# Both heads' transposes and the values at the end of a unit, the second head's blocks in the values' PSUM bank

## Chip, cores and metric

The kernel runs on one core of one Trainium2 chip. The metric is the device time of one execution in microseconds (us), the median of three runs: 1748.26 us for the kernel before. The time of the kernel after is measured in the same way.

## What is computed

A two-layer hybrid encoder takes one step on 512 new prompt frames and 32 sample frames. In each layer one large input projection feeds three branches (a gated convolution, a gated token mixer and stick-breaking attention), their outputs are merged, and a gated feed-forward part follows. The change touches the attention alone:

```python
def stick_breaking(q, k, v, q_pos, k_pos):
    z = jnp.einsum('bqhd,bkhd->bhqk', q, k, preferred_element_type=jnp.float32) * (SB_HEAD_DIM ** -0.5)
    mask = k_pos[None, :] < q_pos[:, None]
    log_keep = jnp.where(mask, jax.nn.log_sigmoid(-z), 0.0)
    later = lax.cumsum(log_keep, axis=3, reverse=True) - log_keep
    attn = jnp.where(mask, jnp.exp(jax.nn.log_sigmoid(z) + later), 0.0)
    return jnp.einsum('bhqk,bkhd->bqhd', attn.astype(v.dtype), v)

def stick_breaking_prompt(q, k, v):
    ...
    for i in range(seq // SB_QBLOCK):
        lo, hi = i * SB_QBLOCK, (i + 1) * SB_QBLOCK
        outs.append(stick_breaking(q[:, lo:hi], k[:, :hi], v[:, :hi], pos[lo:hi], pos[:hi]))
    return jnp.concatenate(outs, axis=1)
```

A prompt has four query blocks of 128 rows, and block i sees i + 1 key blocks. There are eight heads of width 64. The kernel works on them in four pairs.

## The kernel before

**The main work.** TensorE multiplies activations by weight chunks. Each float32 product is made from a high and a low part, so each tile takes three matmuls: high by high, low by high, high by low (lines 2046, 2051 and 2052, in the helper `three_of`). A *unit* is one accumulation into one of the four PSUM banks `acc0` to `acc3`: 8 tiles by 3 matmuls, 24 matmuls of 272 columns. A *chunk* of weights gives four units (function `chunk`, which calls `unit`). The helper `unit` calls `mid` after its first 12 matmuls, and `chunk` calls `end` after a unit's last one.

**Attention hidden between units.** In each layer, five chunks in a row (20 units, n = 0 to 19) carry the attention. One *step* is one query block of one pair of heads: 16 steps, where step n belongs to pair n // 4 and has n % 4 + 1 key blocks of 128. Then two steps for the sample rows follow. A step goes through the engines as follows:

- TensorE, `scores(n)` at the end of unit n: the scores of both heads into the banks `score0` and `score1` (line 2122).
- ScalarE, `sigmoids(n)` in unit n + 1: two sigmoids for each head, `keep` and `beta` (lines 644 and 645). Every second step has its `beta` in the buffer that is called `gex`.
- GpSimd masks the diagonal block, two instructions for each head (line 543).
- VectorE, `made(n)` in unit n + 1: for each head a scan along `keep` (line 1347) and a product into `beta` (line 1350), which signals `at_full` of that head.
- TensorE, `turns(n, part)` in unit n + 2: transposes of the first head's blocks (`part` 0) in the middle of the unit, in `within`, and of the second head's (`part` 1) at its end, in `behind`. Both go to one PSUM bank, `turned` (`bt`, line 2153), so part 1 waits for ScalarE's copy of part 0 (`att_full`).
- ScalarE, `turned(n, part)`: copies out of that bank into `att` and `late` (lines 663 and 666).
- TensorE, `values(ht)`, once for each pair of heads, in the middle of the units n = 6, 10, 14 and 18: eight matmuls into the whole bank `small` (`bo`, 512 columns, line 2173).
- ScalarE, `out_rows(ht)`, right behind its first copy of that unit: copies `small` to the high part of the branch's result (line 681).
- VectorE, `rows_lo(ht)`, in unit n = 7, 11, 15 and 19: reads `small` once more for the low part (line 1370) and signals `yc_full`. In units 7, 11 and 15 it stands in VectorE's queue behind `made(6)`, `made(10)` and `made(14)`, both heads of a step with three blocks; the function `attend` sets that order. The next `values` waits for `yc_full`, since it writes the same bank.

**What sets the order.** Each engine's order is written out by hand, and an engine takes its instructions in that order. A wait on a semaphore holds up all that stands behind it on its engine. On TensorE that is everything: the units, the transposes and the scores are one queue.

Of the kernel before, what the change touches and what calls it, by code (L numbers as in the profile page):

```python
# [8 lines left out]
ACT = mybir.ActivationFunctionType  # L9
AX_X = mybir.AxisListType.X  # L10

P = 128
# [9 lines left out]
CT = CH // P  # L22
# [116 lines left out]
def trunk(nc, adds, x_in, win, wbr, wout, wup, wdn, par_in, bc_in, sguw_in, kc_in, vc_in, gh_in, fh_in,  # L139
          y_out, k_out, v_out, glu_out, ffn_out, sgu_out):  # L140
    with ExitStack() as ctx:
        sems = {}

        def sem(name):
            sems[name] = ctx.enter_context(nc.semaphore(name))
            return sems[name]
# [4 lines left out]
        def sb(name, shape, dt=F32, at=None):  # L151
            size = 4
            for s in shape[1:]:
                size *= s
            off = at
            if at is None:
                off = top[0]
                top[0] += (size + 31) // 32 * 32
            return nc.alloc_sbuf_tensor_at(name, shape, dt, offset=off)
# [9 lines left out]
        ident = sb("ident", [P, P])  # L169
# [70 lines left out]
        beta = [[sb(f"beta0{i}", [P, T], at=C + i * 2176) for i in range(2)],  # L240
                [gex[:, i, 4:GEX] for i in range(2)]]
# [16 lines left out]
        bt = ctx.enter_context(nc.psum_tensor("turned", [P, 512], F32))  # L258
        bo = ctx.enter_context(nc.psum_tensor("small", [P, 512], F32))
# [29 lines left out]
        at_full = [sem(f"at_full{i}") for i in range(2)]  # L289
        t_full = sem("t_full")  # L290
        att_full = [sem(f"att_full{i}") for i in range(2)]
        o_full = sem("o_full")
        o_hi = sem("o_hi")
        yc_full = sem("yc_full")
# [69 lines left out]
        STEPS = 16  # L364
        ALL = STEPS + 2

        def dcol(h):
            return slice(h * HALF, (h + 1) * HALF)
# [3 lines left out]
            return gex[:, b // 2, 4 + b % 2 * HALF:4 + (b % 2 + 1) * HALF]  # L372

        cbank = (bo, bt)
        PA, PB, PC = (ps[0], ps[1]), (bs[0], bs[1]), (bo, bt)

        def bank_of(q, p):
# [196 lines left out]
        def _(act):  # L574
            c = Count()
# [80 lines left out]

            def turned(n, part):

                act.wait_ge(t_full, c.take(t_full))
                if n < STEPS:  # L660
                    i = n % 4
                    early = min(i + 1, 2)
                    ins = A(att[part][:, i:i + 3 * early - 2:3, :],
                            bt[:, 0:early * P].rearrange("p (a n) -> p a n", a=early), ACT.Copy)
                    if i > 1:
                        ins = A(late[part][:, i - 2:2 * i - 3, :],
                                bt[:, 2 * P:(i + 1) * P].rearrange("p (a n) -> p a n", a=i - 1), ACT.Copy)
                    ins.then_inc(att_full[part], c.up(att_full[part]))
                elif part == 0:
                    s = n - STEPS  # L670
                    A(att[s][:, 0:4, :], bt[:, 0:PAST].rearrange("p (a n) -> p a n", a=4), ACT.Copy).then_inc(
                        att_full[s], c.up(att_full[s]))
                else:
                    s = n - STEPS
                    A(att[s][0:DEC, 4, :], bt[0:DEC, 0:P], ACT.Copy).then_inc(att_full[s], c.up(att_full[s]))

            def out_rows(ht):

                act.wait_ge(o_full, c.take(o_full))
                if ht < CT:  # L680
                    A(yc[0][:, ht, 0:SEQ], bo[:, :], ACT.Copy).then_inc(o_hi, c.up(o_hi))
                else:
                    A(yc[0][:, :, SEQ:T], bo[:, 0:P].rearrange("p (a n) -> p a n", a=CT), ACT.Copy).then_inc(
                        o_hi, c.up(o_hi))
# [5 lines left out]
                    sigmoids(n - 1)  # L690

            def within(n):
                if 2 <= n < ALL + 2:
                    turned(n - 2, 0)
                if 6 <= n <= STEPS + 2 and n % 4 == 2:
                    out_rows((n - 6) // 4)

            def behind(n):
                if 2 <= n < ALL + 2:
                    turned(n - 2, 1)  # L700

            def plain(dst, m, b, sig_to, fn=ACT.Copy):

                h = b // 2
                act.wait_ge(acc_full[b], c.take(acc_full[b]))
                A(dst[:, m, dcol(h)], ps[b][:, 0:HALF], fn).then_inc(acc_free[b], c.up(acc_free[b]))
# [1318 lines left out]
        def _(pe):  # L2025
            c = Count()
            mm = pe.matmul
            turn = [0]
            turned_by = [None]
# [11 lines left out]
            def three(out, s, at, xs, start, stop):  # L2041
                return three_of(out, (wh[s][:, at:at + P], wl[s][:, at:at + P]), xs, start, stop)
# [98 lines left out]
            def turn_bank():  # L2141
                if turned_by[0] is not None:
                    pe.wait_ge(turned_by[0], c.seen(turned_by[0]))

            def turns(n, part):
# [15 lines left out]
                c.skip(att_full[s])  # L2161
                turned_by[0] = att_full[s]

            def values(ht):

                for b in range(2):
                    pe.wait_ge(att_full[b], c.seen(att_full[b]))
                pe.wait_ge(yc_full, c.prev(yc_full))
                for kb in range(4):
                    for b in range(2):  # L2170
                        h = 2 * ht + b
                        blocks = (att[b][:, 0:4, :], att[b][:, 4:7, :], late[b][:, 0:2, :], late[b][:, 2:3, :])[kb]
                        last = mm(bo[DH * b:DH * b + DH, kb * P:SEQ], vtok[:, kb, h * DH:(h + 1) * DH],  # L2173
                                  blocks.rearrange("p a n -> p (a n)"), start=kb == 0, stop=kb == 3)
                last.then_inc(o_full, c.up(o_full))
# [18 lines left out]

            def within(n):

                if 6 <= n <= STEPS + 2 and n % 4 == 2:
                    values((n - 6) // 4)
                if 2 <= n < ALL + 2:
                    turns(n - 2, 0)  # L2200

            def behind(n):
                if 2 <= n < ALL + 2:
                    turns(n - 2, 1)
                if n == ALL + 2:
                    sample_values()
                if n < ALL:
                    scores(n)
# [16 lines left out]
            for r in range(DEPTH):  # L2225
# [8 lines left out]
                if r == 0:  # L2234
# [4 lines left out]
                    for t in range(KT):  # L2239
# [3 lines left out]
                        for b in range(2):  # L2243
                            last = three(ps[b][:, 0:HALF], s0, t * 256 + b * P, [x[:, t, dcol(0)] for x in xs],
                                         t == 0, t == KT - 1)
# [57 lines left out]
                for n in range(5):  # L2303
                    if n == 2:
                        qk_out[8] = out_of()
                    chunk(mid=lambda b, n=n: within(4 * n + b), end=lambda b, n=n: behind(4 * n + b))
# [10 lines left out]
                def last_values(b):  # L2317
                    if b == 0:
                        behind(STEPS + 4)
                    turn_first(b)  # L2320
# [81 lines left out]
                blocks = {}  # L2402
# [160 lines left out]
```

## Time and profile before

| | |
|---|---|
| median of 3 runs | 1748.26 us (1747.83 to 1748.93) |
| the profiled execution | 1748.06 us, of it 1746.3 us span |
| TensorE matmul busy | 1732.0 us, 99% of the span |
| VectorE busy | 1331.6 us, 76% |
| ScalarE busy | 850.4 us, 49% |
| GpSimd busy | 122.6 us, 7% |

The span is what the trace covers, and 1.8 us of the execution lie around it. Busy times of one engine can be added; those of different engines overlap. A start time in the rows below counts from the start of the span. A matmul's printed duration is how long it is in the engine; matmuls overlap, so what one costs TensorE is the distance from its start to the start of the next.

### The profile page before, as it was taken

To read this page: it belongs to the slowest core of one execution; us is meant where nothing else is said; L and a number is where in the kernel's file an instruction comes from. 1 tells how busy PE (TensorE), PEld (TensorE's weight loads), DVE (VectorE), ACT (ScalarE), POOL (GpSimd) and SP (SyncE) were. 2 spreads that over 40 slices of the span, in tenths; PEclk is the share of its full clock that TensorE was granted. 3 is DMA by queue.
4 is the path that set the end of the run, shared out by engine and by line. 5 is a ranking of instruction groups with operands and counts; after the bars stand their busy time and mean duration, and the time that the engine had idled before them with its cause. 6 is when DMAs were issued, how large, how long until landed. Compare 5 with 4: busy or idle time off the path is not lost.

```text
span 1746.3 us, 32655 instructions
## 1 busy us (share of the span) xinstructions
PE 1732.0 (99%) x13802; PEld 1697.1 (97%) x13802; DVE 1331.6 (76%) x1903; ACT 850.4 (49%) x1388; POOL 122.6 (7%) x167
## 2 busy tenths in 40 slices
PE   9999999999999999999999999999999999999997
PEld 9998899999999999999999989999999999999997
DVE  5698778664779999876667887777457799998675
ACT  4246532363366655644542565233535556656443
POOL 0025100000030000000000350000001200000000
PEclk9999999999999999999999999999999999999999
DMA  5432132222213223355524221223232222223544
GB/s 177 156 117 74 37 97 75 74 88 94 87 66 114 97 97 100 107 181 176 169 96 156 93 73 62 75 85 96 74 99 95 73 97 97 97 99 131 176 163 136
DMA packets 36513, 185.99 MB, mean 107 GB/s; under 512 B 7376, under 2 KB 11728, under 8 KB 18192
## 3 DMA queue, kind: packets, MB, share of 16 engines
q1 hardware_dynamic: 34672, 176.28, 30.1%
q10 hardware_dynamic: 1696, 7.64, 1.3%
q8 instruction: 109, 1.79, 0.4%
q14 instruction: 36, 0.29, 0.1%
HBM read 176.75 MB, written 7.15 MB: 105 GB/s over the span
## 4 chain that ended last, share of the span: by engine, by line
PE 95%; DVE 3%; issue 1%; DMA 0%; ACT 0%; ACTq 0%; DVEq 0%
PE acc L2046 23%; PE acc L2052 23%; PE acc L2051 23%; PE score L2046 5%; PE score L2052 5%; PE score L2051 5%; PE turned L2051 1%; PE turned L2052 1%; PE score L2122 1%; PE turned L2046 1%; PE small L2051 1%; PE small L2052 1%; PE small L2046 1%; PE small L2173 1%; PE turned L2153 1%; DVE acc L1402 1%
## 5 line engine op out<-in xcount | busy, mean ns | idle before, releaser
L2046 PE MATMUL acc<-xh,wh 128*128 128x272 f32 x1928 | 564.9, 293 | 1.4 <-DVE xl L1152 1.2
L2052 PE MATMUL acc<-xh,wl 128*128 128x272 f32 x1928 | 555.4, 288 | 0.0
L2051 PE MATMUL acc<-xl,wh 128*128 128x272 f32 x1928 | 554.9, 288 | 0.0
L2046 PEld LDWEIGHTS acc<-xh,wh 128*128 128x128 f32 x1928 | 363.1, 188 | 9.1 <-issue 5.4
L1198 DVE TENSOR_TENSOR wl<-raw,wh 128x2048 fp32r<-128x2048 f32 (+2 forms) x118 | 236.1, 2001 | 174.0 <-ACT wh L586 173.4
L2051 PEld LDWEIGHTS acc<-xl,wh 128*128 128x128 f32 x1928 | 363.2, 188 | 0.1
L2052 PEld LDWEIGHTS acc<-xh,wl 128*128 128x128 f32 x1928 | 362.2, 188 | 0.0
L586 ACT ACTIVATE wh<-raw 128x2048 fp32r<-128x2048 f32 (+2 forms) x138 | 236.5, 1714 | 163.8 <-DMA raw<-wdn 116.8
L2046 PE MATMUL acc<-fhh,wh 128*128 128x272 f32 x704 | 204.1, 290 | 0.0
L2052 PE MATMUL acc<-fhh,wl 128*128 128x272 f32 x704 | 202.5, 288 | 0.0
L2051 PE MATMUL acc<-fll,wh 128*128 128x272 f32 x704 | 202.4, 287 | 0.0
L1402 DVE SCALAR_TENSOR_TENSOR acc<-glu,par,acc 128x574 f32<-128x574 f32 x240 | 181.1, 814 | 0.1
L864 ACT ACTIVATE tmp<-acc,par 128x272 f32<-128x272 f32 x96 | 46.7, 488 | 195.1 <-PE acc L2052 194.8
L2046 PEld LDWEIGHTS acc<-fhh,wh 128*128 128x128 f32 x704 | 132.6, 188 | 0.4
L2051 PEld LDWEIGHTS acc<-fll,wh 128*128 128x128 f32 x704 | 132.5, 188 | 0.2
L2052 PEld LDWEIGHTS acc<-fhh,wl 128*128 128x128 f32 x704 | 132.3, 188 | 0.0
L2046 PE MATMUL score<-th,shi 128*128 128x272 f32 x288 | 83.9, 291 | 0.0
L2052 PE MATMUL score<-th,slo 128*128 128x272 f32 x288 | 83.2, 289 | 0.0
L2051 PE MATMUL score<-tl,shi 128*128 128x272 f32 x288 | 82.5, 287 | 0.0
L2046 PE MATMUL acc<-mh,wh 128*128 128x272 f32 x256 | 74.8, 292 | 0.0
L2052 PE MATMUL acc<-mh,wl 128*128 128x272 f32 x256 | 73.7, 288 | 0.0
L2051 PE MATMUL acc<-ml,wh 128*128 128x272 f32 x256 | 73.7, 288 | 0.0
(321 smaller groups left out, 3883.7 us busy)
## 6 DMA issues: line engine op xcount, KB each, us to landing
raw<-win SPq DMA_DIRECT2D x50, 1024.0 KB, 5.0
raw<-wup SPq DMA_DIRECT2D x44, 1024.0 KB, 5.0
raw<-wdn SPq DMA_DIRECT2D x32, 1024.0 KB, 4.9
raw<-wbr SPq DMA_DIRECT2D x24, 512.0 KB, 3.7
raw<-wdn SPq DMA_DIRECT2D x16, 768.0 KB, 4.2
raw<-wout SPq DMA_DIRECT2D x8, 1024.0 KB, 5.1
v_out<-vfm ACTq DMA_DIRECT2D x2, 1088.0 KB, 9.3
k_out<-k ACTq DMA_DIRECT2D x2, 1088.0 KB, 4.9
```

The lines of the kernel that those rows point to most:

```text
L586: A(wh[s][:, 0:n], raw[s][:, 0:n], ACT.Copy).then_inc(hi_full[s], c.up(hi_full[s]))
L864: A(tmp[:, b, :], ps[b][:, 0:HALF], ACT.Sigmoid, bias=col(par, PAR["b_gate"] + 8 * BRANCHES[n] + 2 * i + b % 2)).then_inc(acc_free[b], c.u ...
L1198: v.tensor_tensor(wl[s][:, 0:n], raw[s][:, 0:n], wh[s][:, 0:n].bitcast(F32), ALU.subtract).then_inc(lo_full[s], c.up(lo_full[s]))
L1402: v.scalar_tensor_tensor(out=acc[:, m, :], in0=glu_at(m, j), scalar=w, in1=acc[:, m, :], op0=ALU.mult, op1=ALU.add).then_inc(vec, c.up(vec))
L2046: first = mm(out, a, xs[0], start=start, stop=False, skip_group_check=onto)
L2051: mm(out, a, xs[1], start=False, stop=False, skip_group_check=onto)
L2052: return mm(out, b, xs[0], start=False, stop=stop, skip_group_check=onto)
L2122: last = mm(bs[b][:, 0:w], yc[x][rows, ht, i * P:w], ks[y][rows, ht, 0:w], start=x + y == 0, stop=y == 1)
L2153: last = pe.transpose(bt[:, kb * P:(kb + 1) * P], beta[n % 2][part][:, kb * P:(kb + 1) * P], ident[:, :])
L2173: last = mm(bo[DH * b:DH * b + DH, kb * P:SEQ], vtok[:, kb, h * DH:(h + 1) * DH], blocks.rearrange("p a n -> p (a n)"), start=kb == 0, sto ...
```

## The change

Three things change, in the steps of the prompt (n < 16):

- On TensorE the new function `both_turns` transposes the blocks of both heads, one behind the other, at the end of the unit. The middle of a unit is empty, except in the units 18 and 19. `values` of the pairs 0, 1 and 2 moves from the middle to the end of its unit, ahead of `both_turns`. The last pair's `values` and the sample steps stay in the middle of their units.
- The second head's blocks go to another place: for a step with one block to the second quarter of `turned`, for a step with two, three or four blocks to `small`, the bank of the values (`second_bank`). Before these blocks TensorE waits until `yc_full` has reached the number of the `values` issued so far, the wait `pe.wait_ge(yc_full, c.seen(yc_full))`. The wait for the copy of the first head's blocks between the two heads falls away.
- On ScalarE `turned` of both heads and `out_rows` of the pairs 0 to 2 move to the end of the unit, behind the copies of the unit's own result. Where both heads' blocks lie in one bank, the first copy waits for both heads' transposes.

VectorE's, GpSimd's and SyncE's instructions and their orders are as before.

```diff
             return gex[:, b // 2, 4 + b % 2 * HALF:4 + (b % 2 + 1) * HALF]
 
         cbank = (bo, bt)
+
+        def second_bank(blocks):
+            return (bt, P) if blocks == 1 else (bo, 0)
+
         PA, PB, PC = (ps[0], ps[1]), (bs[0], bs[1]), (bo, bt)
 
         def bank_of(q, p):
@@ -656,15 +660,16 @@
 
             def turned(n, part):
 
-                act.wait_ge(t_full, c.take(t_full))
+                act.wait_ge(t_full, c.take(t_full) + (1 if n < STEPS and n % 4 == 0 and part == 0 else 0))
                 if n < STEPS:
                     i = n % 4
                     early = min(i + 1, 2)
+                    bank, at = second_bank(i + 1) if part else (bt, 0)
                     ins = A(att[part][:, i:i + 3 * early - 2:3, :],
-                            bt[:, 0:early * P].rearrange("p (a n) -> p a n", a=early), ACT.Copy)
+                            bank[:, at:at + early * P].rearrange("p (a n) -> p a n", a=early), ACT.Copy)
                     if i > 1:
                         ins = A(late[part][:, i - 2:2 * i - 3, :],
-                                bt[:, 2 * P:(i + 1) * P].rearrange("p (a n) -> p a n", a=i - 1), ACT.Copy)
+                                bank[:, 2 * P:(i + 1) * P].rearrange("p (a n) -> p a n", a=i - 1), ACT.Copy)
                     ins.then_inc(att_full[part], c.up(att_full[part]))
                 elif part == 0:
                     s = n - STEPS
@@ -690,14 +695,18 @@
                     sigmoids(n - 1)
 
             def within(n):
-                if 2 <= n < ALL + 2:
+                if STEPS + 2 <= n < ALL + 2:
                     turned(n - 2, 0)
-                if 6 <= n <= STEPS + 2 and n % 4 == 2:
-                    out_rows((n - 6) // 4)
+                if n == STEPS + 2:
+                    out_rows(CT - 1)
 
             def behind(n):
+                if 2 <= n < STEPS + 2:
+                    turned(n - 2, 0)
                 if 2 <= n < ALL + 2:
                     turned(n - 2, 1)
+                if 6 <= n < STEPS + 2 and n % 4 == 2:
+                    out_rows((n - 6) // 4)
 
             def plain(dst, m, b, sig_to, fn=ACT.Copy):
 
@@ -2161,6 +2170,23 @@
                 c.skip(att_full[s])
                 turned_by[0] = att_full[s]
 
+            def both_turns(n):
+
+                blocks = n % 4 + 1
+                for part in range(2):
+                    pe.wait_ge(at_full[part], c.take(at_full[part]))
+                    if part == 0:
+                        turn_bank()
+                    elif blocks > 1:
+                        pe.wait_ge(yc_full, c.seen(yc_full))
+                    bank, at = second_bank(blocks) if part else (bt, 0)
+                    for kb in range(blocks):
+                        last = pe.transpose(bank[:, at + kb * P:at + (kb + 1) * P],
+                                            beta[n % 2][part][:, kb * P:(kb + 1) * P], ident[:, :])
+                    last.then_inc(t_full, c.up(t_full))
+                    c.skip(att_full[part])
+                turned_by[0] = att_full[1]
+
             def values(ht):
 
                 for b in range(2):
@@ -2194,13 +2220,17 @@
 
             def within(n):
 
-                if 6 <= n <= STEPS + 2 and n % 4 == 2:
+                if n == STEPS + 2:
+                    values(CT - 1)
+                if STEPS + 2 <= n < ALL + 2:
+                    turns(n - 2, 0)
+
+            def behind(n):
+                if 6 <= n < STEPS + 2 and n % 4 == 2:
                     values((n - 6) // 4)
-                if 2 <= n < ALL + 2:
-                    turns(n - 2, 0)
-
-            def behind(n):
-                if 2 <= n < ALL + 2:
+                if 2 <= n < STEPS + 2:
+                    both_turns(n - 2)
+                if STEPS + 2 <= n < ALL + 2:
                     turns(n - 2, 1)
                 if n == ALL + 2:
                     sample_values()
```

The change moves instructions, so here is what stands in TensorE's queue at the end of the first pair of heads, in the first layer. Units 6 and 7 before (`acc` is a unit's own work, cut here; `beta` is step 4, `gex` step 5):

```order
L2052 MATMUL acc<-xh,wl_58 128x272
L2173 MATMUL small<-att_141,vtok 64x512 [waits yc_full,att_full1,att_full0]
...
L2153 MATMUL turned<-ident,beta_139 128x128 [waits att_full1,at_full0]
L2046 MATMUL acc<-xh,wh_52 128x272
...
L2153 MATMUL turned<-ident,beta_140 128x128 [waits att_full0,at_full1]
L2122 MATMUL score<-ksh,ych 128x384 [waits sig_full1,sig_full0]
...
L2153 MATMUL turned<-ident,gex 128x128 [waits att_full1,at_full0]
...
L2153 MATMUL turned<-ident,gex 128x128 [waits att_full0,at_full1]
...
L2122 MATMUL score<-ksh,ych 128x512 [waits sig_full1,sig_full0]
```

The same place of the changed kernel, whose line numbers are higher:

```order
L2199 MATMUL small<-att_141,vtok 64x512 [waits yc_full,att_full1,att_full0]
...
L2184 MATMUL turned<-ident,beta_139 128x128 [waits att_full1,at_full0]
L2184 MATMUL turned<-ident,beta_140 128x128 [waits at_full1]
L2131 MATMUL score<-ksh,ych 128x384 [waits sig_full1,sig_full0]
...
L2184 MATMUL turned<-ident,gex 128x128 [waits att_full1,at_full0]
L2184 MATMUL turned<-ident,gex 128x128
L2184 MATMUL small<-ident,gex 128x128 [waits yc_full,at_full1]
L2184 MATMUL small<-ident,gex 128x128
L2131 MATMUL score<-ksh,ych 128x512 [waits sig_full1,sig_full0]
```

The values and all transposes now stand between a unit's last matmul and the scores, and the second head's transposes of unit 7 write `small` behind a wait for `yc_full`.

ScalarE's queue from the end of unit 5 to the sigmoids of step 6, before:

```order
L645 ACTIVATE gex<-score 128x256
L663 ACTIVATE att_141<-turned 128x128 [waits t_full]
L681 ACTIVATE ych<-small 128x512 [waits o_full]
L796 ACTIVATE qd<-acc 128x32 [waits acc_full2]
L798 ACTIVATE ych<-acc 128x240
L663 ACTIVATE att_142<-turned 128x128 [waits t_full]
L644 ACTIVATE keep_137<-score 128x384 [waits at_full0,s_full0]
```

and in the changed kernel:

```order
L649 ACTIVATE gex<-score 128x256
L805 ACTIVATE qd<-acc 128x32 [waits acc_full2]
L807 ACTIVATE ych<-acc 128x240
L668 ACTIVATE att_141<-turned 128x128 [waits t_full]
L668 ACTIVATE att_142<-turned 128x128 [waits t_full]
L686 ACTIVATE ych<-small 128x512 [waits o_full]
L648 ACTIVATE keep_137<-score 128x384 [waits at_full0,s_full0]
```

Both copies of step 4 and the copy of `small` now stand right ahead of the sigmoids of step 6.

VectorE's queue, the same in both kernels, at the same place:

```order
L1347 SCALAR_TENSOR_TENSOR keep_137<-keep_137,zero 128x384 [waits mask_full0]
L1350 TENSOR_TENSOR beta_139<-beta_139,keep_137 128x384 [waits vec]
L1347 SCALAR_TENSOR_TENSOR keep_138<-keep_138,zero 128x384 [waits mask_full1]
L1350 TENSOR_TENSOR beta_140<-beta_140,keep_138 128x384 [waits vec]
L1370 TENSOR_TENSOR ycl<-small,ych 128x512 [waits o_hi]
```

The read of `small` stands behind both heads of step 6.

## Rows read from the trace of the kernel before

**Rows 1.** The page: busy time by engine, and granted TensorE clock in 40 slices.
```profile
PE 1732.0 (99%) x13802; PEld 1697.1 (97%) x13802; DVE 1331.6 (76%) x1903; ACT 850.4 (49%) x1388; POOL 122.6 (7%) x167
PEclk9999999999999999999999999999999999999999
```
**Rows 2.** Waits of PE alone: line, releaser, total us, times, longest us.
```profile
PE acc L2046 <- DVE xl L1152: 1.2, 2, 1.0
```
**Rows 3.** PE timeline, unit 2's middle (start us, us, instruction): one transpose.
```profile
116.07 0.29 PE L2052 MATMUL acc<-xh,wl 128*128 128x272 f32 x1
...
116.44 0.28 PE L2051 MATMUL acc<-xl,wh 128*128 128x272 f32 x1
116.56 0.29 PE L2052 MATMUL acc<-xh,wl 128*128 128x272 f32 x1
```
**Rows 4.** PE timeline, ends of units 1 (no transpose) and 2 (one transpose).
```profile
113.83 0.29 PE L2052 MATMUL acc<-xh,wl 128*128 128x272 f32 x1
114.05 0.39 PE L2122 MATMUL score<-ksh,ych 64*128 64x256 f32 x2
...
117.69 0.29 PE L2052 MATMUL acc<-xh,wl 128*128 128x272 f32 x1
117.82 0.27 PE L2153 MATMUL turned<-ident,beta 128*128 128x128 f32 x1
118.02 0.44 PE L2122 MATMUL score<-ksh,ych 64*128 64x384 f32 x2
```
**Rows 5.** PE timeline, unit 5: four transposes in the middle, four at the end.
```profile
129.12 0.29 PE L2052 MATMUL acc<-xh,wl 128*128 128x272 f32 x1
...
129.81 0.28 PE L2051 MATMUL acc<-xl,wh 128*128 128x272 f32 x1
...
131.06 0.30 PE L2052 MATMUL acc<-xh,wl 128*128 128x272 f32 x1
...
131.73 0.38 PE L2122 MATMUL score<-ksh,ych 64*128 64x256 f32 x2
```
**Rows 6.** PE timeline, unit 6: values and one transpose in its middle.
```profile
133.75 0.29 PE L2052 MATMUL acc<-xh,wl 128*128 128x272 f32 x1
133.97 1.72 PE L2173 MATMUL small<-att,vtok 128*64 128x512 f32 x8
...
136.27 0.33 PE L2153 MATMUL turned<-ident,beta 128*128 128x128 f32 x1
...
136.56 0.28 PE L2051 MATMUL acc<-xl,wh 128*128 128x272 f32 x1
```
**Rows 7.** PE timeline: scores of step 6, then the transposes at unit 7's end.
```profile
138.14 0.44 PE L2122 MATMUL score<-ksh,ych 64*128 64x384 f32 x2
...
142.21 0.38 PE L2153 MATMUL turned<-ident,gex 128*128 128x128 f32 x2
```
**Rows 8.** DVE timeline in unit 7: scans of step 6, and the read of `small`.
```profile
140.89 1.02 DVE L1347 TENSOR_TENSOR_SCAN keep<-keep,zero 128x384 f32<-128x384 f32 x1 [1.85 <-POOL beta L543]
...
143.88 0.68 DVE L1370 TENSOR_TENSOR ycl<-small,ych 128x512 fp32r<-128x512 f32 x1
```
**Rows 9.** PE timeline, the same place of unit 11.
```profile
162.38 0.38 PE L2153 MATMUL turned<-ident,gex 128*128 128x128 f32 x2
```
**Rows 10.** DVE timeline, the read of `small` in unit 11.
```profile
163.95 0.68 DVE L1370 TENSOR_TENSOR ycl<-small,ych 128x512 fp32r<-128x512 f32 x1
```
**Rows 11.** ACT timeline, unit 6 into unit 7: copies, and the first sigmoid.
```profile
136.63 0.28 ACT L663 ACTIVATE att<-turned 128x128 f32<-128x128 f32 x1 [2.83 <-PE turned L2153]
136.81 0.59 ACT L681 ACTIVATE ych<-small 128x512 fp32r<-128x512 f32 x1
...
138.97 0.49 ACT L644 ACTIVATE keep<-score 128x384 f32<-128x384 f32 x1 [0.20 <-PE score L2122]
```
**Rows 12.** PE timeline at the start: TensorE's longest wait.
```profile
9.99 0.36 PE L2046 MATMUL acc<-xh,wh 128*128 128x272 f32 x1 [0.99 <-DVE xl L1152]
```
**Rows 13.** DVE timeline at the start: the instruction that ended that wait.
```profile
9.12 0.72 DVE L1152 TENSOR_TENSOR xl<-xT,xh 128x544 fp32r<-128x544 f32 x1
```

More of the change, by code:

```diff
@@ L2195, in within @@
             def within(n):
-                if 6 <= n <= STEPS + 2 and n % 4 == 2:
-                    values((n - 6) // 4)
-                if 2 <= n < ALL + 2:
+                if n == STEPS + 2:
+                    values(CT - 1)
+                if STEPS + 2 <= n < ALL + 2:
                     turns(n - 2, 0)
             def behind(n):
-                if 2 <= n < ALL + 2:
+                if 6 <= n < STEPS + 2 and n % 4 == 2:
+                    values((n - 6) // 4)
+                if 2 <= n < STEPS + 2:
+                    both_turns(n - 2)
+                if STEPS + 2 <= n < ALL + 2:
                     turns(n - 2, 1)
```

## Prediction

> **What bounds the kernel now.** I read the page first. TensorE is busy for 1732.0 us, 99% of the span of 1746.3 us, and its granted clock reads full in all 40 slices [rows 1]. Then TensorE's waits: its largest row is 1.2 us in two waits at the start [rows 2], the three rows under it are smaller, and none is at a transpose of attention, at the values or at the scores of L2122. So the kernel is TensorE's queue. A us less of work in it is a us gained, a wait put into it is a us lost, and no later wait is there that could give it back. VectorE, at 76%, counts only where TensorE waits for it. The third view is the timeline of TensorE through the attention units, to see what a transpose costs in the middle of a unit and at its end. The last is the timelines of VectorE and ScalarE in units 6 and 7, where the new wait stands.
>
> **What the moved transposes give.** Two successive matmuls of a unit start 0.12 to 0.13 us apart, I take 0.125 [rows 3]. In the middle of unit 2 one transpose stands between an L2052 and the next but one matmul, which come 116.44 - 116.07 = 0.37 us apart instead of 0.25: it costs 0.12 us. Four transposes in unit 5 cost 129.81 - 129.12 - 0.25 = 0.44 us [rows 5]. At a unit's end the distance to the scores is 0.22 us with no transpose and 0.33 us with one [rows 4], 0.67 us with four [rows 5]: 0.11 and 0.45 us. So a block costs 0.11 us in either place, and breaking into a unit costs next to nothing beyond that: 0.01 us or less. There are 16 steps in each of 2 layers, 32 breaks, so this gives 0 to 0.3 us; I take 0.2 us.
>
> The values cost 136.56 - 133.75 - 0.25 = 2.56 us in the middle of unit 6 with their one transpose [rows 6]. At the end, the same eight pairs take 136.27 - 133.97 = 2.30 us, the way in is 0.22 us instead of the 0.13 us that a transpose there has (117.69 to 117.82, [rows 4]), and the transpose is 0.11 us: 2.50 us. That gives 0.06 us for each of 6 (three pairs of heads, two layers), 0.4 us. The gain on TensorE is 0.6 us in all, with bounds of 0 and 1.0 us.
>
> The dropped wait for ScalarE's copy between the heads gives nothing, since TensorE did not wait at a transpose [rows 2]. ScalarE's copies that now come later are wanted by TensorE a whole unit later (about 3 us), when the values or the next first-head transposes need them; that unit hides them.
>
> **What the new wait costs.** This is the large term. The second head's transposes of a step with two or more blocks write `small`, so they wait for `yc_full`, for VectorE's read of the values (L1370). The first such step behind a `values` is in the next unit: values in unit 6, transposes of step 5 (two blocks) at the end of unit 7. Before, that bank had until the next `values`, in unit 10. VectorE's place for the read is unchanged: behind both scans and products of step 6. These start only when the scores of step 6 have been through ScalarE and GpSimd; VectorE itself waits 1.85 us for that in unit 7 [rows 8]. So the read can't come earlier because TensorE waits; it hangs on scores that TensorE issued one unit before.
>
> Measured in the trace of before: the scores of step 6 start at 138.14 and the transposes at unit 7's end at 142.21 [rows 7]. In the changed kernel the second head's transposes would come at the same distance from the scores, since the two transposes that leave the unit's middle stand in front of them now. The read ends at 143.88 + 0.68 = 144.56 [rows 8]. TensorE is 144.56 - 142.21 = 2.35 us too early. In unit 11 it is 163.95 + 0.68 - 162.38 = 2.25 us [rows 9, 10]. The other four places (unit 15, and units 7, 11 and 15 of the second layer) repeat this, with 2.24, 2.24, 2.25 and 2.24 us. Sum of six: 13.6 us.
>
> Two things are added at each place. First, ScalarE: the last transpose of unit 6 starts 0.20 us ahead of the scores [rows 4]; the copy behind it starts 0.36 us later (136.27 to 136.63, [rows 6, 11]), that is at scores + 0.16. Then come 0.18 us for one copy, 0.18 us for the other head's, and the copy of `small`, 0.59 us, of which about 0.1 us overlaps with the next instruction (as 136.63 + 0.28 runs past 136.81, [rows 11]). The first sigmoid starts at scores + 1.01 us; before it started at 138.97 - 138.14 = 0.83 us. All behind it, GpSimd's masks, the scans and the read, is 0.18 us later. Bounds: 0 (if the overlap is larger) and 0.3 us. Second, TensorE's start after VectorE's end, which no transpose shows; the nearest row is the wait at the start, where VectorE ends at 9.12 + 0.72 = 9.84 and TensorE starts at 9.99 [rows 12, 13]: 0.15 us. The Trainium skill, "Advanced Engine Details and Errata", section Network/Comms, gives 50 to 100 ns for reading a semaphore; by that the sum would be 0.3 to 0.6 us smaller, and the row decides. Bounds from the rows: 0 and 0.3 us, since the printed 0.68 us of the read may hold some of it.
>
> So a place costs 2.68 us in unit 7 of the first layer and about 2.58 us in the five others, 13.6 + 6 x 0.33 = 15.6 us in all. Behind the waiting transpose stand the scores of step 7 and all the units, so nothing on TensorE covers it.
>
> **Sum.** 1748.06 us (the profiled execution, 1746.3 us of it span; 0.2 us under the median) - 0.6 + 15.6 = 1763.1 us; I say 1763.0 us, 0.84% slower. With all bounds at one end: -1.0 + 13.6 = +12.6, 1760.7 us; at the other: 0 + 13.6 + 6 x 0.6 = +17.2, 1765.3 us.
>
> **Rivals.**
>
> *The clock falls.* TensorE would stand still for some 2.6 us six times, and in this trace it never waits over 1.2 us [rows 2], around which the clock reads full [rows 1]. So no row shows what such a pause does. If the engine went from 2.4 to 1.2 GHz for about a unit behind each pause, 24 matmuls at 0.125 us more, 3.0 us, would be added six times: 1763 + 18 = 1781 us. For one pause alone it is 1766 us. Against it stands that each pause is short beside the full work around it. The Trainium skill, "TensorE: Matmul & The Clock Gate", section "HAM oscillation", has idle stretches between bursts of matmuls bring the lower clock back; no row here bears it out. Chance 0.10.
>
> *No wait, so not slower.* If VectorE's read had ended before TensorE reaches the bank, only the gain would be left: 1748.1 - 0.6 = 1747.5 us, no difference that can be measured. The mechanism would be a read that goes ahead of the scans of step 6, or sigmoids that start much sooner because the ScalarE queue is shorter in the middle of unit 7. It decides at 142.21: the read would have to end 2.35 us sooner. VectorE's queue has not changed, and it already waits for GpSimd there [rows 8]. The same result comes about if the wait asks for a lower count than I read. Chance 0.04.
>
> *A second wait behind the first.* After the pause the scores of step 7 (four blocks) come 2.6 us late, and their transposes stand at the end of unit 9. From the scores of step 6 to the end of its products is 143.88 - 138.14 = 5.7 us [rows 7, 8], for four blocks about 1.1 us more by the width of its instructions, 6.9 us. TensorE needs two units of 3.1 us, two sets of scores and six transposes, about 8.3 us. The slack of 1.4 us covers it. If it were gone, up to 1 us at each of six places would be added: 1769 us. Chance 0.05.
>
> **How the numbers follow.** The forecast of 1763 us, bounds 1760 to 1766, has 0.80. The clock has 0.10, the second wait 0.05, no wait 0.04, and 0.01 is left for a gain that I don't see. A measurement of this kernel tells a difference of about 0.2% (3.5 us) from none. Slower by more than that: 0.80 + 0.10 + 0.05 = 0.95. Within it: 0.04. Faster: 0.01. The range goes from 1757 (waits shorter than the rows' lower bound) to 1770 us (it takes in the second wait and a lower clock after one or two pauses), and leaves out the clock's full price and the case of no wait.
>
> **What would show it.** In the profile of the changed kernel TensorE's waits should have a row for the transposes into `small`, released by VectorE L1370, six times (more with lesser ones), about 15 us in total, 2.7 us at most. VectorE's scan of step 6 should still wait for GpSimd, and the read end about 0.2 us later against the scores than before. A unit without a break should take 24 matmuls at 0.125 us. The granted clock should stay full in every slice; a lower digit in slices 4, 5, 24 or 25 is the first rival. If the transposes into `small` show no wait, the reading of the counts or of VectorE's order was wrong, and if the pauses are there but the time is not, something on TensorE was cheaper without the breaks than the distances in [rows 3 to 6] say.

## The result, and the profile after

The changed kernel takes 1774.01 us (median of 4 runs, 1771.91 to 1776.71) against 1748.6 us, a ratio of 1.0149 (95% interval 1.0137 to 1.0161). It is slower by 25.4 us, where 14.9 us was forecast, and it lies outside the range that was given. Its profiled execution took 1774.42 us, 1772.7 us of it span; that is 26.4 us more span than before. A few executions of the versions below, and of the kernel before beside them, took 2022 to 4341 us; they are left out of every median and ratio here.

The page of the kernel after, busy time by engine and granted TensorE clock in 40 slices, answers to [rows 1]:

```profile
PE 1743.2 (98%) x13802; PEld 1704.9 (96%) x13802; DVE 1331.3 (75%) x1903; ACT 848.3 (48%) x1388; POOL 115.6 (7%) x167
PEclk9999999999999999999999998999999999999999
```

TensorE has the same 13802 matmuls and is busy for 11.2 us longer. So the loss is not idle time alone: the same work took longer. A single 8 stands in the row of the clock, in the 25th slice. A slice is 44 us wide and a 9 stands for 90% or more, so the row is too coarse for the sign that the prediction named: slices 4, 5 and 24 read 9, though the clock was low for 3.4 us in each of them, twice in the 4th, as the stretches further down show.

TensorE's waits (line, releaser, total us, times, longest us), which answer to [rows 2]:

```profile
PE small L2184 <- DVE ycl L1379: 14.2, 6, 2.5
PE acc L2055 <- DVE xl L1161: 1.8, 2, 1.5
```

The first row is the forecast wait: the transposes into `small` (L2184), released by VectorE's read (now L1379), six times. The second row is the wait at the start that was there before, 0.6 us longer in this execution. One small row further down matters for the account at the end, a single wait for a weight chunk at 735 us, which the kernel before did not have in its trace:

```profile
PE score L2055 <- DVE wl L1814: 0.4, 1, 0.4
```

The timeline of TensorE from the end of unit 7 into unit 8 (start us, us, instruction), which answers to [rows 7]:

```profile
142.25 0.29 PE L2061 MATMUL acc<-xh,wl 128*128 128x272 f32 x1
142.38 0.38 PE L2184 MATMUL turned<-ident,gex 128*128 128x128 f32 x2
145.22 0.41 PE L2184 MATMUL small<-ident,gex 128*128 128x128 f32 x2 [2.46 <-DVE ycl L1379]
145.56 0.70 PE L2131 MATMUL score<-ksh,ych 64*128 64x512 f32 x2
...
148.11 0.43 PE L2060 MATMUL acc<-xl,wh 128*128 128x272 f32 x1
148.34 0.43 PE L2061 MATMUL acc<-xh,wl 128*128 128x272 f32 x1
...
149.31 0.28 PE L2060 MATMUL acc<-xl,wh 128*128 128x272 f32 x1
149.44 0.29 PE L2061 MATMUL acc<-xh,wl 128*128 128x272 f32 x1
...
150.96 0.29 PE L2061 MATMUL acc<-xh,wl 128*128 128x272 f32 x1
```

The first head's two transposes take 0.22 us from 142.38. The second head's could start at 142.60 and start at 145.22: a pause of 2.62 us. At 148.11 two matmuls of a unit are 0.23 us apart, at 149.31 they are 0.13 us apart again. Both are the same instruction; between them the clock has come back.

The same seen as stretches (stretch, then its length, busy time of each engine with instructions in brackets, granted clock, DMA share, GB/s), the first six at or behind the end of the six pauses and the last elsewhere:

```profile
core 0: us, PE busy (x) PEld busy (x) DVE busy (x) ACT busy (x) POOL busy (x), PEclk, DMA share, GB/s
145.70:149.10 3.40, 3.40 (x15) 2.66 (x16) 0.57 (x3) 2.31 (x6) 0.54 (x2) 0.50 0.22 34
169.60:173.00 3.40, 3.40 (x15) 2.43 (x14) 1.09 (x2) 1.88 (x5) 0.27 (x2) 0.50 0.07 12
193.50:196.90 3.40, 3.34 (x13) 2.29 (x14) 1.36 (x2) 1.46 (x4) 0.00 (x0) 0.50 0.00 0
1020.80:1024.20 3.40, 3.40 (x25) 2.83 (x26) 1.16 (x3) 2.45 (x6) 0.54 (x2) 1.00 0.26 36
1043.40:1046.80 3.40, 3.32 (x13) 2.27 (x14) 1.39 (x2) 1.43 (x4) 0.00 (x0) 0.50 0.02 5
1067.30:1074.10 6.80, 6.50 (x27) 5.46 (x28) 3.81 (x6) 4.24 (x6) 2.23 (x4) 0.50 0.40 126
1098.00:1101.40 3.40, 3.40 (x19) 3.36 (x17) 3.33 (x5) 0.28 (x1) 0.00 (x0) 0.50 0.00 0
```

A clock of 0.50 is 1.2 GHz, 1.00 is 2.4 GHz. At five of the six pauses the clock went to the low level, at one of those for twice as long; after the pause in unit 7 of the second layer (1020.80) it stayed full. Compare the instructions in equal stretches: 15 matmuls at half clock, 25 at full. The stretch at 1098.00 follows no pause. Ahead of it stand 3.3 us of the sample rows' small matmuls, 32 columns each, which TensorE has in every version.

### The profile page after: what moved, and what is told of

Same layout as the page of the kernel before. It is cut to its first block, busy times and chain, and to the rows that moved or that the text cites. A ratio compares the mean times of both kernels' runs of the same rounds, so it can differ in the third digit from the quotient of the medians.

```text
span 1772.7 us, 32647 instructions
## 1 busy us (share of the span) xinstructions
PE 1743.2 (98%) x13802; PEld 1704.9 (96%) x13802; DVE 1331.3 (75%) x1903; ACT 848.3 (48%) x1388; POOL 115.6 (7%) x167
## 4 chain that ended last, share of the span: by engine, by line
PE 92%; DVE 4%; ACT 1%; issue 1%; DMA 1%; POOL 0%; ACTq 0%; DVEq 0%; POOLq 0%
PE acc L2055 22%; PE acc L2061 22%; PE acc L2060 22%; PE score L2055 5%; PE score L2061 4%; PE score L2060 4%; PE turned L2060 1%; PE turned L2061 1%; PE score L2131 1%; PE turned L2055 1%; PE small L2060 1%; PE small L2061 1%; PE small L2055 1%; PE small L2199 1%; DVE acc L1411 1%
## 5 line engine op out<-in xcount | busy, mean ns | idle before, releaser
L1356 DVE TENSOR_TENSOR_SCAN keep<-keep,zero 128x128 f32<-128x128 f32 (+4 forms) x68 | 58.3, 857 | 37.9 <-POOL gex L547 18.7
```

The lines of the kernel that those rows point to most:

```text
L1356: v.tensor_tensor_scan(keep[b][:, T - w:T][:, ::-1], keep[b][:, T - w:T][:, ::-1], zero[:, 0:1].broadcast_to([P, w]), 1.0, ALU.mult, ALU.a ...
```

## Experiments

There were two theories. **A:** the pauses are VectorE's late read of `small`, and the rest is the lower clock that the pauses bring. **B:** the moved transposes, values and copies themselves cost the part that the pauses don't explain. All ratios below are to the kernel before on the same chip.

### e1: the two-block steps leave `small` alone

```diff
         def second_bank(blocks):
-            return (bt, P) if blocks == 1 else (bo, 0)
+            return (bt, blocks * P) if blocks < 3 else (bo, 0)
...
-                act.wait_ge(t_full, c.take(t_full) + (1 if n < STEPS and n % 4 == 0 and part == 0 else 0))
+                act.wait_ge(t_full, c.take(t_full) + (1 if n < STEPS and n % 4 < 2 and part == 0 else 0))
...
-                    elif blocks > 1:
+                    elif blocks > 2:
                         pe.wait_ge(yc_full, c.seen(yc_full))
```

> The changed kernel, but a step with two blocks puts the second head's blocks in the free half of the bank turned, so only steps with three or four blocks write small. Theory A (the loss is the wait for VectorE's read of small in units 7, 11 and 15 of both layers, and the lower clock that follows the pauses): no wait is left, the first write to small behind the values comes a unit later, and the time falls from 1774 to the kernel before less the small gain, 1747 to 1748.5 us. Rival B (the moved transposes, values and ScalarE copies themselves cost the part that the pauses don't explain, some 10 us): 1756 to 1760 us.

Measured: ratio 1.0001 (0.9992 to 1.001), median 1748.54 us against 1748.14 us. The same work is moved, the values included, and the whole loss of 25.4 us is gone. That rejects B. TensorE's waits have no row for attention's transposes any more; the largest is the one at the start:

```profile
PE acc L2055 <- DVE xl L1161: 1.3, 1, 1.3
```

### e2: VectorE reads `small` first

```diff
             def attend(n):
...
+                if 7 <= n < STEPS + 3 and n % 4 == 3:
+                    rows_lo((n - 7) // 4)
                 if 1 <= n <= ALL:
                     made(n - 1)
-                if 7 <= n <= STEPS + 3 and n % 4 == 3:
+                if n == STEPS + 3:
                     rows_lo((n - 7) // 4)
```

> The changed kernel with its banks as they are, but VectorE reads small ahead of the scans of steps 6, 10 and 14 instead of behind them. Theory A: ScalarE's copy of small is done long before TensorE comes to its transposes, VectorE was idle there anyway, so the pauses and the lower clock vanish: 1747 to 1748.5 us. Rival B: about 1758 us. Rival C (the bank small is late for another reason than VectorE's order, for example ScalarE's copy): still 1770 us or more.

Measured: ratio 0.9999 (0.999 to 1.0007), median 1747.94 us. Banks and TensorE's queue are those of the changed kernel, and one instruction of VectorE in another place takes the whole loss away. Rival C falls with it. The timeline of VectorE in unit 7, which answers to [rows 8]:

```profile
139.41 0.69 DVE L1379 TENSOR_TENSOR ycl<-small,ych 128x512 fp32r<-128x512 f32 x1 [0.90 <-ACT ych L686]
141.19 1.02 DVE L1356 TENSOR_TENSOR_SCAN keep<-keep,zero 128x384 f32<-128x384 f32 x1 [1.09 <-POOL beta L547]
```

The read is done at 140.10, more than 2 us ahead of the transposes at 142.38, and lies in time in which VectorE waited anyway.

### e3: the wait alone, in the kernel before

```diff
             def turns(n, part):
...
                 turn_bank()
+                if n < STEPS and part == 1 and n % 4:
+                    pe.wait_ge(yc_full, c.seen(yc_full))
                 if n < STEPS:
```

> The kernel before, all work in its old place and bank, plus the one wait of the changed kernel: the second head's transposes of steps with two or more blocks wait for VectorE's read. Theory A: six pauses of about 2.35 to 2.5 us, 14 to 15 us, and the lower clock after most of them, 8 to 10 us more: 1771 to 1775 us. Rival B: only the pauses, 1762 to 1764 us.

Measured: ratio 1.014 (1.0127 to 1.0153), median 1772.79 us, 24.7 us more than before. No instruction is moved; one wait makes nearly the whole loss of 25.4 us. TensorE's waits show 13.5 us for it, and this time the clock fell at all six pauses. First the wait, then the stretch after the first pause:

```profile
PE turned L2155 <- DVE ycl L1370: 13.5, 6, 2.3
```

```profile
144.80:151.70 6.90, 6.59 (x28) 5.54 (x28) 3.50 (x6) 3.11 (x8) 2.23 (x4) 0.51 0.39 133
```

### e4, e8 and e9: idle matmuls in the pause

The delay stays, but TensorE works through part of it. The results of these matmuls are read by nobody; they stand behind ScalarE's last read of that bank.

```diff
                     elif blocks > 1:
+                        if blocks == 2 and n > 4:
+                            for b in range(2):
+                                pe.wait_ge(sig_full[b], c.seen(sig_full[b]))
+                            for _ in range(20):
+                                mm(bs[0][:, 0:HALF], xh[:, 0, 0:P], xh[:, 0, dcol(0)], start=True, stop=True)
                         pe.wait_ge(yc_full, c.seen(yc_full))
```

e8 has 10 in place of the 20, e9 has 5.

> The changed kernel with 20 idle matmuls of 272 columns (2.5 us of work whose result nobody reads) ahead of each of the six waits, so that TensorE works through the pause and waits at most 0.2 us. Theory A (the pause costs 15.2 us and the clock about 10 us): the clock stays full and the time is 1762 to 1765 us. Rival B: the clock has little to do with it, 1772 us or more.

> The changed kernel with 10 idle matmuls of 272 columns (1.25 us) ahead of each wait, half as many as fill the pause: TensorE's empty time is about 1.35 us at each of six places, the same as in the version with the read between the heads, while the total delay stays at 2.6 us. If 1.3 us of emptiness leaves the clock full: 1763 to 1765 us, as with the pause filled. If it brings the lower clock: 1772 us or more.

> The changed kernel with 5 idle matmuls (0.6 us) ahead of each wait, so TensorE stands empty for about 1.9 us at each of six places; with 10 (1.3 us empty) the clock stayed full at all six, with none (2.5 us) it fell at five. If 1.9 us is still short enough everywhere: 1763 to 1765 us. If it brings the lower clock at every place: 1772 to 1774 us. In between, at some places: 1766 to 1771 us.

Measured: 20 matmuls 1764.26 us, ratio 1.0091 (1.0078 to 1.0104); 10 matmuls 1764.26 us, ratio 1.0091 (1.0075 to 1.0107); 5 matmuls 1768.91 us, ratio 1.0113 (1.0095 to 1.0131). In the version with 20 the scores behind the pause run at their usual pace, and TensorE's waits have no row for L2189:

```profile
142.12 0.38 PE L2189 MATMUL turned<-ident,gex 128*128 128x128 f32 x2
142.25 2.75 PE L2185 MATMUL score<-xh 128*128 128x272 f32 x20
144.87 0.44 PE L2189 MATMUL small<-ident,gex 128*128 128x128 f32 x2
145.24 0.50 PE L2131 MATMUL score<-ksh,ych 64*128 64x512 f32 x2
```

So the delay alone is worth 16.1 us (1764.26 - 1748.14), near the 15.2 us of the pauses, and filling it with useless work saves 9.8 us against the changed kernel (9.3 us, when each is compared with the kernel before beside it: 25.4 - 16.1). This is the price of the clock. With 10 matmuls TensorE stood empty for 1.2 to 1.3 us at each place (from the start of the last idle matmul to the transpose, less the usual 0.125 us; the printed waits are 6.2 us in six) and the clock stayed full at all six; in that execution it fell once, for 3.4 us, near the sample rows' small matmuls:

```profile
1088.90:1092.30 3.40, 3.40 (x18) 3.40 (x17) 3.17 (x5) 0.12 (x1) 0.00 (x0) 0.50 0.02 5
```

With 5 it stood empty for 1.8 to 1.9 us (printed: 9.9 us in six), and the clock fell at five of the six places. The one that escaped is in unit 11 of the first layer, as the stretches of that version show (same columns as above):

```profile
125.00:150.00 25.00, 23.24 (x170) 19.75 (x169) 18.86 (x29) 14.31 (x39) 10.48 (x19) 0.93 0.26 86
150.00:175.00 25.00, 23.37 (x183) 19.99 (x183) 19.04 (x27) 14.02 (x40) 9.66 (x17) 1.00 0.29 107
175.00:200.00 25.00, 23.37 (x176) 19.63 (x175) 20.13 (x29) 13.55 (x38) 9.95 (x16) 0.93 0.13 43
```

### e5: the values back in the middle

This is e1 with `values` of all pairs and `out_rows` in `within`, where they stood before. It has one measured execution.

```diff
             def within(n):
-                if n == STEPS + 2:
-                    values(CT - 1)
+                if 6 <= n <= STEPS + 2 and n % 4 == 2:
+                    values((n - 6) // 4)
```

> The changed kernel with two-block steps in the bank turned (no pause), and the values and ScalarE's copy of small back in the middle of their unit; the transposes of both heads stay at the end. It splits the small gain, which the trace of the version without pauses shows as 0.26 us where 0.6 us was forecast. If the values' move gave the 0.4 us of the forecast, TensorE's distance over the two attention stretches grows by about that; if it gave nothing, by under 0.1 us. The time alone can't tell: 1747 to 1749 us.

Measured: 1748.49 us. The distance from one matmul ahead of the attention stretch to one behind it, the same two in each version (at 109.12 and 215.07 us in the kernel before, in the second layer at 975.02 and 1078.02): before 105.95 + 103.00 us, e1 105.89 + 102.94 us, e5 105.98 + 103.03 us. So the move of both heads' transposes gave nothing (e5 is 0.06 us longer than before, which is near the rounding of the starts), and the move of the values gave 0.18 us. All of the change's gain is 0.12 us, and the trace of e2 has the same two distances as e1. The 0.26 us in the expectation were taken over a longer part of the trace and hold other differences between two executions.

### e6 and e7: VectorE's read sooner and later

e6 puts the read between the first and the second head of step 6 (10, 14), e7 behind the convolution taps of its unit.

```diff
                         weights(b, (n % 4 + 1) * P, beta[n % 2][b], b)
+                        if b == 0 and n % 4 == 2 and n > 4:
+                            rows_lo((n - 6) // 4)
```

```diff
                         if n < 2:
                             taps(1)
+                            if u == 7:
+                                rows_lo(0)
                             qk_lo(4 + n, b)
                         else:
                             taps(TAPS_UNIT[u % 2])
+                            if u in (11, 15):
+                                rows_lo((u - 7) // 4)
```

> The changed kernel, but VectorE reads small between the scans of the first and the second head of steps 6, 10 and 14. The six pauses shrink from 2.6 to 1.0 to 1.3 us each, 7 us in all. Theory A1 (a pause of that length leaves the clock full): about 1755 us. Theory A2 (any pause, however short, can bring the lower clock after it): 10 us more, 1763 to 1766 us. Rival (VectorE's place is not what sets the pause): 1772 us or more.

> The changed kernel, but VectorE's read stands behind the convolution taps of its unit, one tap (0.8 us) in unit 7, two taps (1.6 us) in units 11 and 15. The pauses grow from 2.6 to 3.3 us (2 of them) and 4.1 us (4 of them), 7.8 us more in all. If the clock's price does not depend on the pause's length: 1774 + 8 = 1782 us. If a longer pause brings the lower clock sooner and for longer, so that part of it falls on the pause itself or twice the time behind it: anything from 1778 to 1788 us; the clock's stretches in the profile tell which.

Measured: e6 1753.2 us, ratio 1.0027 (1.0016 to 1.0039); e7 1783.84 us, ratio 1.0204 (1.0186 to 1.0222). TensorE's waits of e6, then of e7:

```profile
PE small L2186 <- DVE ycl L1381: 4.1, 6, 1.0
```

```profile
PE small L2188 <- DVE ycl L1379: 21.5, 6, 3.8
```

e6 costs 4.9 us over before with 4.1 us of waits and a full clock: a pause of 0.8 to 1.2 us costs itself and no more. Theory A1 holds there, at a lower price than I expected, since five of the six pauses were 0.8 us, shorter than the 1.0 us I had put at least. From start to start the six sum to 5.0 us. e7 costs 35.5 us over before. Its waits are 7.3 us longer than the changed kernel's, and it is 9.8 us slower (1783.84 - 1774.01), so the clock's share grew a little, from about 10 to about 13 us (the difference of these two, an estimate). The stretches of e7 say why. At the four longer pauses the low clock lasted twice as long as at most places of the changed kernel, but part of it fell into the pause. The pause in unit 11 of the first layer, its last 1.3 us and what follows it (columns as above):

```profile
169.90:171.20 1.30, 0.00 (x0) 0.00 (x0) 1.21 (x2) 0.00 (x0) 0.00 (x0) 0.50 0.00 0
171.20:176.60 5.40, 5.34 (x22) 4.29 (x23) 1.24 (x2) 3.46 (x6) 1.40 (x4) 0.50 0.29 70
```

### e10: the second bank taken back

```diff
         def second_bank(blocks):
-            return (bt, P) if blocks == 1 else (bo, 0)
+            return (bt, 0)
...
-                act.wait_ge(t_full, c.take(t_full) + (1 if n < STEPS and n % 4 == 0 and part == 0 else 0))
+                act.wait_ge(t_full, c.take(t_full))
...
-                    if part == 0:
-                        turn_bank()
-                    elif blocks > 1:
-                        pe.wait_ge(yc_full, c.seen(yc_full))
+                    turn_bank()
...
-                turned_by[0] = att_full[1]
+                    turned_by[0] = att_full[part]
```

> Both heads' transposes and the values at the end of the unit as in the changed kernel, but the second head's blocks in the bank turned as before, so TensorE waits there for ScalarE's copy of the first head's blocks, and never for VectorE's read. What the second bank is worth: ScalarE's copies take 0.3 us for one or two blocks and 0.6 to 0.7 us for three or four, and with the way to the engine and back TensorE would wait 0.4 to 0.6 us and 0.8 to 1.0 us at 32 places, some 20 us: 1765 to 1773 us, with a full clock. If the copies are ready sooner than that: 1755 to 1765 us.

Measured: 1782.6 us, ratio 1.0195 (1.0179 to 1.0211), 34 us more than before and outside what I expected. TensorE's waits:

```profile
PE turned L2181 <- ACT late L671: 16.5, 16, 1.2
PE turned L2181 <- ACT att L668: 10.6, 16, 1.0
```

They are 27.1 us over 32 places, 0.66 us each for steps with one or two blocks and 1.03 us for three or four. I had put 0.4 to 0.6 and 0.8 to 1.0 us. The printed waits leave out the rest of the way: taken from start to start between the two heads' transposes, less the usual 0.11 us, the 32 places sum to 32.6 us, nearly all of the 34 us; 1.5 us more in the profiled execution are one fall of the clock at 1107 us, away from the waits. One place, three transposes for each head, where 0.33 us would be the distance:

```profile
128.92 0.49 PE L2181 MATMUL turned<-ident,beta 128*128 128x128 f32 x3
130.62 0.52 PE L2181 MATMUL turned<-ident,beta 128*128 128x128 f32 x3 [1.21 <-ACT late L671]
```

So once both heads' transposes stand side by side, a second bank is needed; the trouble was the choice of `small` for the step right behind the values. The clock stayed full at all 32 places, though TensorE waited at each.

## Why the prediction was wrong

**What bounds the kernel: right.** With the waits in place, each microsecond of them was lost, and nothing later gave it back.

**The new wait: right in place, cause, number and size.** It is six waits, released by VectorE's read. The forecast had 2.68 us for the first and 2.58 us for the others. From the timeline, with 0.22 us for the first head's transposes taken off, they are 2.62, 2.50, 2.52, 2.51, 2.50 and 2.52 us, 15.2 us against 15.6 us. Two of the other places, from TensorE's timeline (start to start, less 0.22 us):

```profile
166.67 0.38 PE L2184 MATMUL turned<-ident,gex 128*128 128x128 f32 x2
169.39 0.50 PE L2184 MATMUL small<-ident,gex 128*128 128x128 f32 x2 [2.34 <-DVE ycl L1379]
...
1018.07 0.38 PE L2184 MATMUL turned<-ident,gex 128*128 128x128 f32 x2
1020.80 0.41 PE L2184 MATMUL small<-ident,gex 128*128 128x128 f32 x2 [2.36 <-DVE ycl L1379]
```

The term for TensorE's start after VectorE's end, 0.15 us, was right: the read ends at 144.39 + 0.68 = 145.07, and TensorE starts at 145.22. ScalarE's term was right in its cause and too large: the scores of step 6 start at 138.55 and the first sigmoid at 139.46, 0.91 us later, where 0.83 us was read from before and 1.01 us forecast. That is 0.08 us later and not 0.18, inside the bounds given. The timelines of VectorE and ScalarE:

```profile
144.39 0.68 DVE L1379 TENSOR_TENSOR ycl<-small,ych 128x512 fp32r<-128x512 f32 x1
```

```profile
138.99 0.60 ACT L686 ACTIVATE ych<-small 128x512 fp32r<-128x512 f32 x1
139.46 0.51 ACT L648 ACTIVATE keep<-score 128x384 f32<-128x384 f32 x1
```

**The gain: too large, without weight.** Forecast 0.6 us, measured 0.12 us. The difference of 0.01 us for each break into a unit was within the rounding of the starts (e5 has no gain from it), and the first transpose behind the values costs about 0.16 us at the unit's end, not 0.11.

**The clock: this is where the forecast failed.** The rival named it, with the right mechanism, and gave it a chance of 0.10. The sum put this term at nothing. The argument against it, "each pause is short beside the full work around it", was not read from any row; between its first and its last matmul the trace of before held no wait over 1.2 us, so nothing there priced 2.6 us. But one place of that trace, which the prediction does not name, shows the clock low with TensorE empty. TensorE's last matmul ends at 1735.30 + 0.62 = 1735.92 us, and from 4.0 us later to the end the clock is at the low level (the second fence has the columns of the stretches above):

```profile
1735.30 0.62 PE L2489 MATMUL turned<-gex,mean_d 128*128 128x272 f32 x2
```

```profile
1739.95:1746.30 6.35, 0.00 (x0) 0.00 (x0) 2.80 (x6) 3.43 (x6) 0.00 (x0) 0.50 0.51 175
```

The honest price for something that no row bounds is a chance of its own, nearer to one half, and a range that reaches to its time. The size that I gave it was also wrong, on the other side. I charged a full unit at half pace, 3.0 us for each of six. Measured at the first place: from the start of the transposes into `small` to the last matmul of unit 8 the changed kernel takes 150.96 - 145.22 = 5.74 us, e2, without a pause, 146.60 - 142.38 = 4.22 us, as its rows show:

```profile
142.38 0.38 PE L2186 MATMUL small<-ident,gex 128*128 128x128 f32 x2
...
146.60 0.29 PE L2063 MATMUL acc<-xh,wl 128*128 128x272 f32 x1
```

That is 1.5 us. The clock was low for 3.4 us, and the lost time is a little less than half of that. The changed kernel and e2 have the same 13802 matmuls in the same order, so the starts of each can be compared all along the two traces. Behind the six pauses the distance grows by 1.5, 1.5, 1.5, 0.0, 1.5 and 2.9 us, 8.9 us in all, and by 1.5 us more near the sample rows: 10.4 us, where the rival had 18 us.

**The second wait behind the first: did not come.** TensorE's waits have no row for it. **No wait:** did not come; e1 and e2 show what it would have given, no measurable difference, as priced.

The account, by the same comparison with e2, whose span is that of the kernel before (1746.3 us): 15.2 us of pauses, 8.9 us of lower clock behind them, 1.5 us of lower clock near the sample rows, 0.7 us at the one wait for a weight chunk at 735 us (0.4 us as printed), 0.2 us at the start, 26.5 us; the spans differ by 26.4 us. No run shows that the change causes the last three. The runs separate the first two on the chip: e4 has the delay without the lower clock (16.1 us over before), and e3 has both without the moved work (24.7 us).

## To carry over

When work moves into a buffer that another engine also reads, look up where that read stands in the other engine's queue, and compare its end with the earliest new write: the trace of before gave this wait to within 5%. A pause on TensorE has two prices, its length and the slower work behind it; here 2.5 us of pause cost about 4.0 us ((15.2 + 8.9) / 6), while pauses up to 1.3 us cost their length and no more. Where the wait can't be avoided at once, move the releasing instruction ahead in its own queue (e2), or use a buffer that has no such reader (e1).

## What the runs showed of the hardware

TensorE's granted clock fell from 2.4 to 1.2 GHz depending on how long it had stood empty, and not at each place alike. Empty for 0.8 to 1.3 us at 12 places (e6, e8): never. For 1.8 to 1.9 us at six places (e9): five times. For 2.4 to 2.6 us at 12 places (the changed kernel and e3): eleven times. For 3.2 to 4.0 us at six places (e7): each time. 32 waits of 0.7 to 1.4 us, from start to start less 0.11 us and 5 to 8 us apart within a layer (e10), did not bring it down where they stood. The changed kernel, e8 and e10 each have one fall right behind the sample rows' 32-column matmuls, at 1098, 1089 and 1107 us, with TensorE busy throughout (e10: 6.60 us busy in the 6.60 us ahead of it); the other nine profiled executions, the kernel before and e2 among them, have the same matmuls and no fall there. What makes the difference from one execution to the next was not tried. The times of the changed kernel spread further than those of the one before beside it, 1771.91 to 1776.71 us against 1747.83 to 1749.91 us, and its slowest execution has the lowest mean granted clock of the four (0.990), its fastest the highest (0.993). That the spread comes from the number of falls fits with this, but is not shown, since one execution alone has its trace. The Trainium skill, "TensorE: Matmul & The Clock Gate", section "HAM oscillation", tells of a clock that falls when the engine waits between bursts of matmuls; its example has waits of about 3 to 5 us. The traces agree on the fall and differ on the length: here 1.8 to 1.9 us was enough at five of six places.
